# A layer with 32 experts on one core: the first pair's rows copied ahead of the tables, the extra pass's loads on ScalarE's queue, gate loads released and taken in parts

## The reference

```python
def hier_moe(h, wg_r, bg_r, we_r, be_r, w_gate, w_up, w_down):
    glog = xf @ wg_r + bg_r                      # 4 groups, top-1
    elog = (xf @ we_r + be_r).reshape(N, 4, 8)   # 8 experts per group
    top_v, top_i = lax.top_k(elog_g, 2)          # top-2 inside the group
    gate = softmax(top_v) * g_w
    y = grouped_experts(xf, e_idx, gate, w_gate, w_up, w_down)

def one_block(toks, e):                          # for each expert
    xb = x_pad[toks]
    hb = silu(xb @ w_gate[e]) * (xb @ w_up[e])   # 1024 -> 512
    return hb @ w_down[e]                        # 512 -> 1024
```

## Time and profile before

| what | value |
|---|---|
| median of 3 runs | 1173.98 us |
| profiled execution | 1174.84 us |
| its span in the trace | 1173.1 us |
| TensorE matmul busy | 1035.7 us (88%) |
| VectorE busy | 459.4 us (39%) |
| ScalarE busy | 185.7 us (16%) |
| DMA moved | 277.50 MB |
| chain by engine | TensorE 21%, DMA 19%, VectorE 3%, issue 2% (the part of it that the trace can follow) |

### The profile page before, as it was taken

One profiled execution on the slowest core, in us unless ns is written; L12 is line 12 of the kernel. 1 busy time (PEld: TensorE's weight loads), 2 busy tenths in 40 slices (PEclk: granted clock), 3 DMA queues, 4 the chain that ended last, 5 costly groups with the idle time before them and its releaser, 6 DMA issues. The chain is left out here.

```text
span 1173.1 us, 11480 instructions
## 1 busy us (share of the span) xinstructions
PE 1035.7 (88%) x4528; PEld 538.3 (46%) x4528; DVE 459.4 (39%) x770; ACT 185.7 (16%) x485; POOL 112.0 (10%) x167
## 2 busy tenths in 40 slices
PE   6999999999999999999997599988787489997780
PEld 3577744555445447777655243333332133332330
DVE  4169644653673032023236643322222024432224
ACT  0156233433223001022100000000000001000001
POOL 1200001122016000000000010000000000000002
PEclk9999999999999999999998699988988699998995
DMA  8221120402324333230085399999999989999987
GB/s 252 72 72 68 48 105 1 160 24 81 103 77 144 134 144 144 72 124 20 14 332 213 145 418 429 426 427 428 425 427 427 402 361 426 426 426 429 426 359 249
DMA packets 55396, 277.50 MB, mean 237 GB/s; under 512 B 13232, under 2 KB 15152, under 8 KB 43184
## 3 DMA queue, kind: packets, MB, share of 16 engines
q1 hardware_dynamic: 42928, 262.30, 55.5%
q0 software_dynamic: 5040, 9.45, 2.1%
q10 hardware_dynamic: 7376, 5.03, 1.4%
HBM read 273.34 MB, written 18.61 MB: 249 GB/s over the span
## 5 line engine op out<-in xcount | busy, mean ns | idle before, releaser
L860 PE MATMUL bank<-arena 128*64 128x512 f32 x1568 | 367.2, 627 | 71.3 <-DMA arena<-in_exp_w_up_dram 20.3
L486 PE MATMUL bank<-arena 128*128 128x512 f32 x640 | 285.0, 599 | 2.7 <-DMA arena<-in_w_in_dram 1.9
L860 PEld LDWEIGHTS bank<-arena 128*64 128x64 f32 x1568 | 122.3, 144 | 303.2 <-issue 279.0
L486 PEld LDWEIGHTS bank<-arena 128*128 128x128 f32 x640 | 119.7, 191 | 147.0 <-issue 145.4
L474 PE MATMUL bank<-arena 128*128 128x288 f32 x640 | 156.1, 406 | 0.0
L474 PEld LDWEIGHTS bank<-arena 128*128 128x128 f32 x640 | 121.4, 190 | 33.8 <-issue 0.4
L1293 ACT ACTIVATE arena<-bank 128x512 f32<-128x512 f32 (+6 forms) x135 | 61.5, 492 | 377.8 <-PE bank L486 110.9
L1516 ACT ACTIVATE arena<-bank,arena 128x512 f32<-128x512 f32 x17 | 11.7, 687 | 440.5 <-PE bank L860 440.5
L2008 DVE TENSOR_SCALAR arena<-arena 128x512 f32<-128x512 f32 x17 | 7.3, 427 | 156.9 <-ACT arena L1516 156.9
L2025 DVE SCALAR_TENSOR_TENSOR arena<-bank,arena 128x512 f32<-128x512 f32 x34 | 25.5, 751 | 91.9 <-PE bank L860 85.5
L2010 DVE RECIPROCAL arena<-arena 128x512 f32<-128x512 f32 x17 | 57.0, 3353 | 0.6
(11 more groups left out here) (291 smaller groups left out, 881.8 us busy)
## 6 DMA issues: line engine op xcount, KB each, us to landing
arena<-in_exp_w_gate_dram SPq DMA_DIRECT2D x34, 2048.0 KB, 33.4
arena<-in_exp_w_up_dram SPq DMA_DIRECT2D x32, 2048.0 KB, 32.2
arena<-in_exp_w_down_dram SPq DMA_DIRECT2D x32, 2048.0 KB, 27.5
arena<-in_w_in_dram SPq DMA_DIRECT2D x7, 2048.0 KB, 8.5
out_dram<-arena SPq DMA_DIRECT2D x4, 1024.0 KB, 10.7
arena<-in_w_mem_k_dram SPq DMA_DIRECT2D x2, 2048.0 KB, 10.2
arena<-in_w_mem_v_dram SPq DMA_DIRECT2D x2, 2048.0 KB, 8.6
arena<-in_w_out_dram SPq DMA_DIRECT2D x2, 2048.0 KB, 12.9
```

The source lines that it names most:

```text
L486: ins = mm(b[:, :], x, w[:, k, :], start=k == 0, stop=k == KC - 1)
L860: ins = mm(bank[own, :], x[:, k, own], w[j][:, k, cols], start=k == 0, stop=k == nk - 1)
```

## The change

- VectorE's first copy_rows moves from behind the list arithmetic to right behind order_i. Every copy_rows and turn_rows now signals after each half (four of eight blocks), and the gate and up matmuls wait for each half (from_rows in place of by_both).
- SyncE issues pair 1's down loads in halves, the first when half of pair 0's gate has been read (g_half), the second when all of it has.
- The extra pass's loads are issued by ScalarE, on its DMA queue, inside its own loop of the extra pass. SyncE only reads the number of passes.
- The last pair's gates are loaded and multiplied in quarters too.
- Pair 1's second gate (part 7) is loaded among pair 0's parts. To free its place, xT is one buffer per tile at a new address, tiles 2 and 3 over 0 and 1; two turns of x change places. squares4 moves.
- near_lists becomes near_slots (ahead of the last residual add) and near_values (behind it). A memset of the lists moves behind. ScalarE waits for the lists' one-hots before its first exp, since that writes over what VectorE still reads.

```diff
@@ constants, buffers
-        xT = area(28672, KC, TOK)
-        squares4 = area(33280, 1024)
+        xT = [area(32768 + w, KC, rows) for w, (_, rows) in zip((0, 1024, 0, 1024, 2048), TILES)]
...
+        squares4 = area(OZ + 2048 + 2 * NT * (NE + P), 1024)
@@ TensorE
-            turn_x(3, 0)
             turn_x(2, 1)
-            turn_x(4, 0)
+            turn_x(3, 0)
             router(2, range(KC))
             pe.wait_ge(sel_ready, 1)
             ranks(0, 2)
+            turn_x(4, 0)
             turn_x(3, 1)
...
                 for k in range(KC):
                     ins = tr(pair[:, k // 4, (k % 4) * P:(k % 4 + 1) * P], rows[:, k, :], ident)
-                ins.then_inc(S.tx_full, 1)
+                    if k % 4 == 3:
+                        ins.then_inc(S.tx_full, 1)
...
+            def from_rows(S, n, bank, w, signal, half_read=None):
+                for k in range(KC):
+                    if k % 4 == 0:
+                        pe.wait_ge(S.xT_cp, 2 * n + k // 4 + 1)
+                    for j in range(2):
+                        own = slice(CAP * j, CAP * (j + 1))
+                        ins = mm(bank[own, :], xgT[:, k, own], w[j][:, k, :], start=k == 0, stop=k == KC - 1)
+                    if k == 3 and half_read is not None:
+                        ins.then_inc(half_read, 1)
+                ins.then_inc(signal, 1)
+
+            def from_rows_by_quarters(bank, w, landed, signal):
+                for k in range(KC):
+                    if k % 4 == 0:
+                        pe.wait_ge(SP_.xT_cp, 2 * (PAIRS - 1) + k // 4 + 1)
+                    if k % 2 == 0:
+                        pe.wait_ge(landed[k // 2], 32)
+                    for j in range(2):
+                        own = slice(CAP * j, CAP * (j + 1))
+                        ins = mm(bank[own, :], xgT[:, k, own], w[j][:, k, :], start=k == 0, stop=k == KC - 1)
+                ins.then_inc(signal, 1)
@@ SyncE
             load_part(0, 4, 0)
+            load_part(1, 1, 3)
...
             sp.wait_ge(lg_full, NT)
-            load_part(1, 1, 3)
-            sp.wait_ge(rstd_ready, 12 + NT)
             load_part(1, 2, 2)
...
-            def load_over():
-                sp.wait_ge(meta_ready, 1)
-                passes = sp.value_load(np_i[0:1, 0:1], min_val=0, max_val=OVER // 2)
-                with sp.If(passes > 0):
-                    with sp.Fori(0, passes) as n:
...
-                            sp.dma_start(over_weights[m], weights_of(which, e[m % 2]), cond=need[m % 2] > 0).then_inc(over_ld[m], 16)
-                return passes
...
+                if i == 1:
+                    for half, (signal, n) in enumerate(((g_half, 1), (SP_.g_full, 1))):
+                        sp.wait_ge(signal, n)
+                        ks = slice(2 * half, 2 * half + 2)
+                        for m in (4, 5):
+                            q = part_place(i, m) % NPART
+                            sp.dma_start(part_out[q][:, ks, :], weights_of(2, e[m % 2])[:, ks, :]).then_inc(w_ld[q], 16)
+                for m in range(6 if 1 < i < PAIRS - 1 else 0):
...
-                        over = load_over()
+                        sp.wait_ge(meta_ready, 1)
+                        over = sp.value_load(np_i[0:1, 0:1], min_val=0, max_val=OVER // 2)
...
-                    load_quarters(1, e, over)
-                    load_quarters(2, e, over)
+                    for which in range(3):
+                        load_quarters(which, e, over)
@@ ScalarE
             act.wait_ge(near_std, 1)
+            act.wait_ge(hot_ready, 2)
...
                     def over_pair(n):
+                        e = [act.value_load(meta_i[0:1, bass.ds(2 * n + j, 1)], min_val=0, max_val=NE - 1) for j in range(2)]
+                        need = [act.value_load(need_i[0:1, bass.ds(2 * n + j, 1)], min_val=0, max_val=1) for j in range(2)]
+                        for m in range(6):
+                            which = m // 2
+                            act.wait_ge(reads[which], (OVER_AFTER + 1) * per_pass[which])
+                            act.wait_ge(over_reads[which], n * per_pass[which] + 1)
+                            act.dma_start(over_weights[m], weights_of(which, e[m % 2]), cond=need[m % 2] > 0).then_inc(over_ld[m], 16)
                         act.wait_ge(ocol_ready, n + 1)
@@ VectorE
             v.tensor_copy(order_i, tmp32).then_inc(order_ready, 1)
 
+            copy_rows(SP_, 0)
             n.link(ts(pos, pos, float(CAP), None, ALU.mult))
...
-            copy_rows(SP_, 0)
             all_lists()
```

105 lines of the change are left out of this document (49 added, 56 removed).

## The result

| | before | changed |
|---|---|---|
| median | 1173.99 us (1173.91 to 1176.15, 4 runs) | 1163.91 us (1163.55 to 1165.38, 4 runs) |
| profiled execution | 1174.84 us, span 1173.1 | 1165.38 us, span 1163.6 |

The ratio is 0.9911, 95% interval [0.9898, 0.9923]: faster by 10.1 us, or 0.9%. The forecast was 1160.0 us, within 1157 to 1166. The direction and the order of size are right, but 3.9 us are missing, and the time lies outside the forecast's own range (1157.7 to 1162.8). So there is something to find.

The account below looks back on a forecast made before the run. The second half was taken as an expert-weight stream at its limit (426 GB/s), ending by its start, bytes and idle time. Gains 7.5 + 5.9 + 0.6 = 14.0 us gave 1160.0 us, own range 1157.7 to 1162.8, given range 1157 to 1166.

Parts of the forecast that it names:

- hole one: Stream idle from 655 to 672 us, as the first gate waits for VectorE's late copy; effective stream start 673.6.
- hole two: DMA share 0.63 from 930 to 945 us, as the extra pass waits for its gate; closing it gains 5.9 us.
- I am wrong if: Signs: extra pass still waits for its gate; new gap over 3 us near 685; first exp waits past up half.
- The start: Earlier copied rows and weight loads at the first pairs: stream gains 7.5 us, bounds 5.7 to 8.6.
- TensorE's shift: First pair's matmuls come 6.45 us earlier (5.7 to 7.05): 5.95 from the earlier copy, 0.5 from the clock.
- dry spell ahead of the third pair of loads: Queue empty when pair 0's down half frees buffers at 684.6; stream restarts at 686.4, so it gains 7.5, not 10.2.
- The halved release itself buys little: Issuing pair 1's downs in halves adds little; TensorE's shift plus 1.0 us of slack binds the start's gain.
- the start gains more: Rival: an almost empty queue restarts at once, keeping most of the 10.2 us: gain 16.5, 1157.5 us; chance 10%.
- The clock gain of 0.5: First matmuls: the stretch at 1.2 GHz may shrink from 5.2 to 3.1 us (gain 1.05) or stay; 0.5 taken.
- The loads of the extra pass: On ScalarE's queue they pass SyncE's backlog, gate landing in about 12 us; the pass starts 15.5 earlier, gain 5.9 us.
- The rule that was weighed: DMAs from several engines share the same 16; by it ScalarE's extra-pass loads are worth 0 and the sum 8.1.
- The last gate in quarters: Last pair: gate matmuls start before all of it lands; gain 1.0 less 0.4 for slower loads, 0.6 us (0 to 1.27).

Follow-up runs that it names:

- e6: The changed kernel with the extra pass's loads back on SyncE's queue and the last gate whole, so the start alone: 1166.51 us, ratio 0.9924 to the kernel before.
- e7: The changed kernel with pair 1's down loads issued whole, once all of the first gate has been read: 1166.33 us, ratio 0.9919 to the kernel before.
- e5: The changed kernel itself, timed again as a yardstick: 1163.56 us, ratio 0.9896 to the kernel before.
- e1: The kernel before with only the extra pass's loads issued by ScalarE on its queue: 1172.03 us, ratio 0.998 to the kernel before.
- e2: The changed kernel with the extra pass's loads back in SyncE's queue: 1165.97 us, ratio 0.9927 to the kernel before.
- e10: The kernel before with only the last gate loaded and multiplied in quarters: 1175.01 us, ratio 0.9996 to the kernel before.
- e4: The changed kernel with the last gate loaded and multiplied whole: 1166.67 us, ratio 0.9929 to the kernel before.
- e11: The changed kernel with slots dealt to partitions in another order by a permuted iota, spreading filled slots over groups of four: 1159.7 us, ratio 0.9869 to the kernel before.
- e3: The changed kernel with SyncE waiting before pair 12's loads until all earlier loads have landed: 1166.54 us, ratio 0.9942 to the kernel before.
- e9: The changed kernel with most indirect gathers and scatters replaced by plain 64-row transfers on ScalarE's queue, outputs wrong: 1175.81 us, ratio 1.0006 to the kernel before.

## Why the prediction was right or wrong

**Right in its view.** A stream at its limit sets the end; hole one was to end earlier and hole two to close. Both did, by the steps named: first gate, releases at 661.7, 672.2 and 684.4, ScalarE's loads past SyncE's backlog, the pass behind its copied rows, the last gate behind the pair before without a gap (1107.62). That the time lies within the range that was given, 1157 to 1166, owes something to luck: the sum's own bounds, 1157.7 to 1162.8, miss it. None of the three "I am wrong if" came true. The first exp started at 665.24, released by the gate and not by the one-hots.

**The start: 7.5 forecast, 8.65 measured (e6).** TensorE's shift was right (6.45 against 6.69). What was too dear was the dry spell ahead of the third pair of loads, 2.7 us in the sum (683.7 to 686.4) and 1.4 measured by bytes; these 1.3 us are about the 1.15 by which the term is short, though the interval of e6 (7.4 to 10.6) also holds 7.5. "The halved release itself buys little" is wrong by this, it buys 2.7 to 2.8 (e7). The upper bound has a slip: a restart in 0.8 us instead of 1.8 gives 1.0 and not 0.5, so it should have been 9.05, which holds the 8.65. The rival "the start gains more" had the right mechanism, though not its whole size. The clock gain of 0.5 is nowhere in the profiled execution (16.84 us for the first 64 matmuls against 16.77 before) and 1.4 us in that of e5 (15.36).

**The loads of the extra pass: 5.9 forecast, 2.3 measured alone (e1), 1.9 to 3.6 within the change (e2).** This is the step that failed, by its size. The mechanism held in the main: in e1 the extra gate lands in 13.7 us (forecast 12) and there is no hole. The pass is late against the forecast, though: it starts at 923.34 in e1 (forecast 918.19), and in the changed kernel at 916.55 with the next release at 923.68, where the forecast with the 6.45 us of TensorE's shift taken off is 911.7 and 918.9. The mistake is in "it is 15 x (1 - 0.63) = 5.55 us". A share is a mean over 16 engines, and a load is done when the slowest engine is. Ahead of the hole the engines were 10 us apart, so a good part of the hole was idle time of the engines ahead only, while the laggards caught up; filling it moved that time to the end, where 3.8 us of idle became 7.3 (6.2 in e5). The sum took the tail of before as fixed. The trace of before could have warned me: it holds the sixteen completions of each load, 10.3 us apart ahead of the hole and 1.2 behind it.

The rule that was weighed, of the Trainium skill's "DMA: Bandwidth & Descriptors", section "Issuing engines are not separate DMA queues", does not describe this kernel: only the issuing engine was changed in e1, and the landing went from 38.3 to 13.7 us. Its other section, "Queues, rings and completion order", by which the engines take turns between queues, agrees with that. Turns have a price, though, which the prediction left out: pair 8's down, in SyncE's queue, landed 49.6 us after its issue, and TensorE waited 8.02 us for it. That made the pass late: 4.9 us behind the forecast, and 2.2 in e5 (913.86). The stream still had bytes (a share of 1.00 over 900 to 930 and 1.01 over 930 to 945), so it was not on the path.

**The last gate in quarters: 0.6 forecast, 0.0 alone (e10), 2.1 to 3.9 beside the drift (e4).** Right for the kernel before, and worth more in the changed one for a reason that the prediction didn't have. So the last two terms can't be added: the second keeps the lateness that the third softens. Together they gave 2.95 and not 6.5.

**The sum.** 8.65 + 2.95 = 11.6 us on the chip that held e5 and e6 (1175.16 to 1163.56), 10.1 in the first comparison. Forecast: 14.0. Of the difference of 2.4 the start gives +1.15 and the two later terms -3.55. With the slots spread over the engines (e11) the gain is 1174.95 - 1159.7 = 15.25 us, close to the forecast's 14.0 plus the 1.15 of the start. This fits that the sum would hold without the drift, but it doesn't show it: e11 is set against a kernel before that drifts itself, and its end is 0.9 us less idle than that kernel's (2.9 against 3.8). The kernel before with its slots spread was not run; it would tell. e11 is the fastest of all kernels here.

## What to carry to other kernels

Before you price a hole in a DMA stream by its share, look at how far the engines' completions of one load lie apart: the hole is worth little more than what the slowest engine is idle in it (here 2.3 of 5.9 us), and the rest comes back at the end of the stream. Gathers and scatters whose used slots bunch up on some partitions load the DMA engines unevenly; dealing the slots out over the partitions costs no instruction and here gained 3.2 to 4.9 us. Price the restart of a stream by its bytes too: beside a restart a share near 1 went with 331 GB/s. And price edits of one stream together: those that remove a gap and those that shorten a tail are not independent.

## What the runs showed of the hardware

- With the indirect transfers of this kernel the 16 DMA engines drift apart by 1.4 us a pass at a share of 1.01, and an idle gap brings them together (10.3 to 1.2 us in the kernel before, 11.5 to 1.8 in e3).
- Around the restart of a nearly emptied queue (680 to 688 us) the stream lost 1.4 us by bytes against 426 GB/s, but only 0.6 us by share (changed kernel, e5: 0.89 and 0.97 at 373 and 331 GB/s). From 684 to 685 us e5 has a share of 1.28 at 262 GB/s, so there the share says too much.
- An empty slot of a gather or scatter shows as a packet of 4 bytes in place of one of 4 KB.
- A load of 2 MB on a second queue beside a full first one landed in 14.0 us where it took 38.3 behind the first one's backlog, at the cost of the loads queued in the first (pair 8's down: 49.6 us to landing).
- Plain 64-row transfers on ScalarE's queue in place of the indirect ones took the stream from 427 to 411 GB/s at the same share of 1.01 (e9). The cause is open.
